# First norm with split row copies and later rounding, and block products one PSUM bank at a time, in a hybrid decoder layer

## What is computed

```
xn = rmsnorm(x, ln1_g)
u, v, q, k, va, ga, gb = split(xn @ w_in)
a = gelu(u) * (tril(W_s[g]) @ rmsnorm(gelu(v)) + b[g])      # chunks of 128, 8 groups
b = sliding-window attention(q, k, va)                      # 16 heads, 4 kv heads, window 128, sinks, ALiBi
x = x + (sigmoid(ga) * (a @ w_oa) + sigmoid(gb) * (b @ w_ob)) @ w_out
x = x + square(relu(rmsnorm(x, ln2_g) @ w_up)) @ w_down
y = rmsnorm(x, lnf_g)
```

## Time and profile before

| | us |
|---|---|
| median of 3 runs | 1611.61 |
| lowest, highest | 1609.47, 1617.08 |
| the profiled execution's own time | 1610.56 |
| its span, first to last instruction | 1608.80 |
| TensorE matmul busy | 1552.6 (97%) |
| VectorE, ScalarE, GpSimd busy | 1054.2, 766.0, 180.6 |

### The profile page before, as it was taken

How to read it: one execution, slowest core, us unless ns; L and a number is a source line. 1 busy time by engine, 2 the same in 40 slices (tenths; PEclk the granted TensorE clock), 3 DMA queues, 4 the chain that set the end, 5 groups by cost and what they waited for, 6 DMA issues and landing times.

```text
span 1608.8 us, 28826 instructions
## 1 busy us (share of the span) xinstructions
PE 1552.6 (97%) x12226; PEld 1516.9 (94%) x12226; DVE 1054.2 (66%) x1377; ACT 766.0 (48%) x1159; POOL 180.6 (11%) x206
## 2 busy tenths in 40 slices
PE   5999999999999989999998999999999999999998
PEld 5988888889999989999998999999999999999997
DVE  4465554312768567866777676977697769776875
ACT  6365555522645535555443555533553355335533
POOL 5122222200000010000110040000000000000001
PEclk7999999999999999999999999999999999999999
DMA  7611110132777614545578363545453636363612
GB/s 223 198 29 53 29 29 27 29 118 79 194 241 222 184 28 106 157 106 157 132 235 186 109 148 102 142 120 143 119 145 109 154 112 151 109 147 112 147 51 106
DMA packets 106409, 200.64 MB, mean 125 GB/s; under 512 B 16624, under 2 KB 44272, under 8 KB 98952
## 3 DMA queue, kind: packets, MB, share of 16 engines
q1 hardware_dynamic: 89344, 127.64, 23.9%
q0 software_dynamic: 10384, 64.00, 20.4%
q10 hardware_dynamic: 6552, 7.13, 1.4%
HBM read 121.77 MB, written 19.30 MB: 88 GB/s over the span
## 4 chain that ended last, share of the span: by engine, by line
PE 85%; DVE 4%; ACT 4%; DMA 3%; issue 2%; POOL 1%; SPq 1%; ACTq 0%; DVEq 0%; POOLq 0%
PE ps L1542 68%; PE ps L1334 10%; PE ps L1322 2%; ACT prob L746 1%; PE ps L1380 1%; DVE prob L1011 1%; DMA h_t<-h_keep 1%; DMA raw<-in_w_in 1%; PE ps L1398 1%; POOL prob L564 1%; DVE y_t L1311 1%; PE ps L1520 1%; DVE w_lo L961 1%; DMA cv<-in_cache_v_win 1%; DVE q_st L991 0%
## 5 line engine op out<-in xcount | busy, mean ns | idle before, releaser
L1542 PE MATMUL ps<-xp_hi,wp_hi 128*128 128x258 f32 x3136 | 634.4, 284 | 6.8 <-DVE wp_lo L1115 6.1
L1542 PE MATMUL ps<-xp_lo,wp_hi 128*128 128x258 f32 x3136 | 635.6, 284 | 0.0
L1542 PE MATMUL ps<-xp_hi,wp_lo 128*128 128x258 f32 x3136 | 634.5, 284 | 0.0
L1542 PEld LDWEIGHTS ps<-xp_hi,wp_hi 128*128 128x128 f32 x3136 | 490.2, 191 | 7.9 <-DVE wp_lo L1115 6.7
L1542 PEld LDWEIGHTS ps<-xp_hi,wp_lo 128*128 128x128 f32 x3136 | 489.8, 190 | 0.0
L1542 PEld LDWEIGHTS ps<-xp_lo,wp_hi 128*128 128x128 f32 x3136 | 486.8, 190 | 0.0
L682 ACT ACTIVATE wp_hi<-wbuf 128x1024 fp32r<-128x1024 f32 x196 | 208.0, 1061 | 549.7 <-PE ps L1542 549.4
L1115 DVE TENSOR_TENSOR wp_lo<-wbuf,wp_hi 128x1024 fp32r<-128x1024 f32 x196 | 243.7, 1243 | 167.1 <-ACT wp_hi L682 167.1
L1334 PE MATMUL ps<-xn_hi,w_hi 128*128 128x344 f32 x480 | 160.8, 335 | 2.5 <-DVE q_st L991 2.5
L1334 PE MATMUL ps<-xn_lo,w_hi 128*128 128x344 f32 x480 | 155.9, 325 | 0.0
L1334 PE MATMUL ps<-xn_hi,w_lo 128*128 128x344 f32 x480 | 155.8, 324 | 0.0
(11 more groups left out here) (191 smaller groups left out, 1555.0 us busy)
## 6 DMA issues: line engine op xcount, KB each, us to landing
wbuf<-wbuf POOLq DMA_DIRECT2D x57, 1024.0 KB, 7.5
wbuf<-in_w_up SPq DMA_DIRECT2D x24, 1024.0 KB, 5.5
wbuf<-in_w_down SPq DMA_DIRECT2D x24, 1024.0 KB, 5.1
wbuf<-in_w_in SPq DMA_DIRECT2D x18, 1024.0 KB, 5.8
raw<-in_w_in SPq DMA_DIRECT2D x40, 256.0 KB, 3.4
wbuf<-in_w_ob SPq DMA_DIRECT2D x6, 1024.0 KB, 7.4
wbuf<-in_w_oa SPq DMA_DIRECT2D x6, 1024.0 KB, 5.0
wbuf<-in_w_out SPq DMA_DIRECT2D x6, 1024.0 KB, 10.8
```

What stands on the lines that cost most here:

```text
L1542: last = mm(ps[:, 2 * p + b, 0:HN], w[:, (2 * n + p // 2) % 2, k, p % 2 * P:(p % 2 + 1) * P], x[n % 2][:, k, b * HN:(b + 1) * HN], start=( ...
```

## The change

In the first norm, tiles go around two pairs of PSUM banks (2 to 5) in place of three (0 to 5). ScalarE copies the first four of a tile's eight blocks and VectorE the other four, with a semaphore of its own that TensorE, GpSimd and the store of `x_t` also wait for. VectorE goes: copy of tile t, scaling of t - 1, `xn_lo` of t - 2. ScalarE goes: square and copy of t, `xn_hi` of t - 2; `w_hi` of job 0 comes one tile earlier. TensorE's spread of a tile comes two tiles after its transposes, and banks 0 and 1 of job 0 are made in halves among the last transposes and spreads. In SyncE's queue `g2`, the sinks and the `raw` pieces of job 1 come after the first three stores. In `product` the loop over the two banks is the outermost.

```diff
+        KA = KT // 2
+        def turned(t):
+            first = 2 + 2 * (t % 2)
+            return ps[:, first:first + 2, :].rearrange("p a (k q) -> p (a k) q", q=P)
...
# SyncE
-            with nc.allow_non_contiguous_dma(reason="gains to partitions, 4 KB each"):
-                for dst, src in ((g2, ln2_g[0]),):
-                    sp.dma_start(dst[:, :], src.rearrange("(k p) -> p k", p=P)).then_inc(small_in, 16)
-            sp.dma_start(nsink[:, :], sinks.to_broadcast([P, H])).then_inc(small_in, 16)
...
+                if g == 0:
+                    for t in range(3):
+                        keep_xn(t)
                 load_block(j + 1, 1 - s, w_in, 0, g * 2 * P + OQ)
                 if g == 0:
-                    for t in range(NTOK):
-                        r = ROWS[t]
-                        sp.wait_ge(xn_ready, t + 1)
-                        sp.dma_start(xn_keep[:, toks(t)].rearrange("(k p) t -> p k t", p=P),
-                                     xg[:, t % 3, :, 0:r]).then_inc(xn_kept[t % 3], 16)
+                    with nc.allow_non_contiguous_dma(reason="gains to partitions, 4 KB"):
+                        sp.dma_start(g2[:, :], ln2_g[0].rearrange("(k p) -> p k", p=P)).then_inc(small_in, 16)
+                    sp.dma_start(nsink[:, :], sinks.to_broadcast([P, H])).then_inc(small_in, 16)
+                    for t in range(3, NTOK):
+                        keep_xn(t)
# GpSimd
                 pool.wait_ge(xt_moved, t + 1)
+                pool.wait_ge(xt_moved_v, t + 1)
# ScalarE
-                copy(x_t[:, :, toks(t)], ps[:, first:first + 2, :].rearrange("p a (k q) -> p (a k) q", q=P)[:, :, 0:r]).then_inc(xt_moved, 1)
-                if t >= 1:
-                    high(t - 1)
-                if t == NBLK - 3:
+                copy(x_t[:, 0:KA, toks(t)], turned(t)[:, 0:KA, 0:r]).then_inc(xt_moved, 1)
+                if t >= 2:
+                    high(t - 2)
+                if t == 4:
                     w_high(0)
+            high(NTOK - 2)
             high(NTOK - 1)
+            act.wait_ge(xt_moved_v, NTOK)
# VectorE
+            def copy_xt(t):
+                dve.wait_ge(xt_done, t + 1)
+                cp(x_t[:, KA:KT, toks(t)], turned(t)[:, KA:KT, 0:ROWS[t]]).then_inc(xt_moved_v, 1)
...
+            for t in range(NTOK):
+                copy_xt(t)
+                if t >= 1:
+                    scale_x(t - 1)
+                if t >= 2:
+                    low(t - 2)
+                if t == 4:
                     split_lo(0, 0)
+            scale_x(NTOK - 1)
+            low(NTOK - 2)
+            low(NTOK - 1)
# TensorE
-                if t >= 3:
-                    spread(t - 3)
-                    pe.wait_ge(xt_moved, t - 2)
+                if t >= 2:
+                    pe.wait_ge(xt_moved, t - 1)
+                    pe.wait_ge(xt_moved_v, t - 1)
                 for k in range(KT):
-                    last = turn(ps[:, first + k // 4, (k % 4) * P:(k % 4) * P + r], x_stage[0:r, t, k * P:(k + 1) * P], r)
+                    last = turn(turned(t)[:, k, 0:r], x_stage[0:r, t, k * P:(k + 1) * P], r)
                 last.then_inc(xt_done, 1)
-            spread(NTOK - 3)
-            pe.wait_ge(xt_moved, NTOK - 2)
-            bank(0, 0, 0, 0, ready=3)
+                if t >= 2:
+                    spread(t - 2)
+                if t >= 7:
+                    bank(0, 0, 0, 0, ready=3, ks=range((t - 7) * KT // 2, (t - 6) * KT // 2))
             spread(NTOK - 2)
+            bank(0, 1, 0, 1, ready=6, ks=range(KT // 2))
             spread(NTOK - 1)
+            bank(0, 1, 0, 1, ks=range(KT // 2, KT))
             pe.wait_ge(xt_moved, NTOK)
+            pe.wait_ge(xt_moved_v, NTOK)
...
-            for n in range(1, 3 * NT):
+            for n in range(2, 3 * NT):
...
-                for k in range(MH):
-                    if p == 0 and k % 2 == 0:
-                        pe.wait_ge(xp_split, 2 * n + k // 2 + 1)
-                    for m, (w, x) in enumerate(passes):
-                        for b in range(2):
+                for b in range(2):
+                    for k in range(MH):
+                        if p == 0 and b == 0 and k % 2 == 0:
+                            pe.wait_ge(xp_split, 2 * n + k // 2 + 1)
+                        for m, (w, x) in enumerate(passes):
                             last = mm(ps[:, 2 * p + b, 0:HN], w[:, (2 * n + p // 2) % 2, k, p % 2 * P:(p % 2 + 1) * P],
```

More of the change, by code:

```diff
@@ L242, in build_trunk @@
         sq_done, rstd_done, rstd_spread = sem("sq_done"), sem("rstd_done"), sem("rstd_spread")
-        xt_done, xt_moved, x_kept = sem("xt_done"), sem("xt_moved"), sem("x_kept")
+        xt_done, xt_moved, xt_moved_v, x_kept = (sem(n) for n in ("xt_done", "xt_moved", "xt_moved_v", "x_kept"))
         xg_done, xn_ready, xhi_done, xn_done = sem("xg_done"), sem("xn_ready"), sem("xhi_done"), sem("xn_done")
@@ L408, in load_block, with keep_xn @@
                 load(j, s, [(raw[:, s, h * KT // 2:(h + 1) * KT // 2, :], halves[h]) for h in (1, 0)])
+            def keep_xn(t):
+                sp.wait_ge(xn_ready, t + 1)
+                sp.dma_start(xn_keep[:, toks(t)].rearrange("(k p) t -> p k t", p=P),
+                             xg[:, t % 3, :, 0:ROWS[t]]).then_inc(xn_kept[t % 3], 16)
             for g in range(NG):
@@ L705, in _ @@
             for t in range(NTOK):
-                r, first = ROWS[t], 2 * (t % 3)
+                r = ROWS[t]
                 act.wait_ge(x_in[t], 16)
@@ L961, in split_lo, with scale_x, low @@
                 tt(w_lo[:, s], raw[:, s], w_hi[:, s].bitcast(F32), ALU.subtract).then_inc(w_split, 1)
-            for t in range(NTOK):
-                r = ROWS[t]
+            def copy_xt(t):
+                dve.wait_ge(xt_done, t + 1)
+                cp(x_t[:, KA:KT, toks(t)], turned(t)[:, KA:KT, 0:ROWS[t]]).then_inc(xt_moved_v, 1)
+            def scale_x(t):
                 dve.wait_ge(xg_done, t + 1)
                 dve.wait_ge(rstd_spread, t + 1)
-                x_ = xg[:, t % 3, :, 0:r]
-                tt(x_, x_, ps[:, 6 + t % 2, 0:r].unsqueeze(1).to_broadcast([P, KT, r]), ALU.mult).then_inc(xn_ready, 1)
+                x_ = xg[:, t % 3, :, 0:ROWS[t]]
+                tt(x_, x_, ps[:, 6 + t % 2, 0:ROWS[t]].unsqueeze(1).to_broadcast([P, KT, ROWS[t]]), ALU.mult).then_inc(xn_ready, 1)
+            def low(t):
                 dve.wait_ge(xhi_done, t + 1)
-                tt(xn_lo[:, :, toks(t)], x_, xn_hi[:, :, toks(t)].bitcast(F32), ALU.subtract).then_inc(xn_done, 1)
-                if t == NBLK - 4:
+                tt(xn_lo[:, :, toks(t)], xg[:, t % 3, :, 0:ROWS[t]], xn_hi[:, :, toks(t)].bitcast(F32), ALU.subtract).then_inc(xn_done, 1)
+            for t in range(NTOK):
[5 more added lines that the diff above has]
+                if t == 4:
                     split_lo(0, 0)
+            scale_x(NTOK - 1)
+            low(NTOK - 2)
+            low(NTOK - 1)
             def bank_low(n):
@@ L1322, in turn, with bank @@
                 return nc.tensor.transpose(out, in_, ident[0:r, 0:r])
-            def bank(j, n, s, b, ready=None):
+            def bank(j, n, s, b, ready=None, ks=range(KT)):
                 if b == 0:
@@ L1331, in bank @@
                     pe.wait_ge(bank_free, n + 1)
-                for k in range(KT):
+                for k in ks:
                     for p, (w, x) in enumerate(((w_hi, xn_hi), (w_hi, xn_lo), (w_lo, xn_hi))):
@@ L1335, in bank @@
                                   start=(k == 0 and p == 0), stop=(k == KT - 1 and p == 2))
-                last.then_inc(bank_done if b < NT - 1 else job_done, 1)
+                if k == KT - 1:
+                    last.then_inc(bank_done if b < NT - 1 else job_done, 1)
             def spread_rstd(place_, t):
```

## The result

The changed kernel takes 1603.64 us, the median of five runs (1599.37 to 1604.26), against 1611.61 (1609.13 to 1617.08) for five of the kernel before: a ratio of 0.9945, with a 95% interval from 0.9927 to 0.9964, or 8.9 us less by the ratio (the medians stand 8.0 apart). The profiled execution took 1599.37 us, its span 1597.6. The forecast was 1606.6 in a range from 1590 to 1618. The gain is 0.55%, with an interval on both sides of 0.5%, so it lies on the edge between the prediction's "same" (0.60) and "faster" (0.30).

A forecast was written before the change was run, and what follows sets the result against it. The prediction took TensorE's own matmul rate as the bound. First norm -4.5, earlier wait +0.5 and loop order 0 gave -4.0 us against the profiled 1610.56: 1606.6 us, in a range from 1590 to 1618.

The forecast's parts named there:

- The products' loop order: Product matmuls (L1542), 9408 steps of 120.5 ns: step time taken as unchanged, 0 us, with -24 and +9 for the range.
- a: Input projection (L1334), 344 columns into one bank: its 14.0 ns surplus would make a product step 121.5 ns, +9 us.
- b: L1380, 256 columns, eight matmuls in two banks with one change of bank: 120.0 ns a step, 120.8 for 258 columns.
- c: Input projection's (L1334) surplus growing with the columns instead: a product step of 118.0 ns, 2.5 cheaper, -24 us.
- one bank is cheaper: Rival on the products' matmuls: smaller surplus per column in one bank, 1583 us at -24 us in full; chance 0.28.
- one bank is dearer: Rival on the products' 9408 steps: 1.0 ns more each, 1615.6 us, or 1625 at twice that; chance 0.10 of passing 0.5%.
- The earlier wait at k = 2: Products: xp_lo's second piece needed after 6 matmuls, not 12, so a covered wait now costs some 0.3 us; +0.5 us.
- The first norm: Norm stage of about 44 us: last scaling 4.5 us sooner, near 39, passing undiminished to job 2; -4.5 us.
- the start: First norm: tile 0's store goes out near 12.3 as small transfers move behind the first three stores; xg of tile 8 2.7 earlier.
- the 7 us that VectorE's own sum promised: First norm: VectorE alone at 3.1 us a tile would end near 37, not 43.6; not taken, because GpSimd shares the port.
- The end: First norm: only tile 6's low part stands before tile 8's scaling, which came 3.3 us after its xg began; 1.8 less.
- the norm isn't shortened: Rival on the first norm: half banks at half clock and moved transfers hold VectorE as long as xn_hi did; 1611, chance 0.14.

The follow-up runs named there:

- order_k_bank_pass: The changed kernel with the products' loops nested k, bank, pass instead of bank, k, pass; 1607.51 us, 120.34 ns a step by the window.
- shifted_operand: The changed kernel with the moving operand's buffer of every second product 32 bytes further on in SBUF; 1599.42 us in one run.
- old_order_one_bank: The changed kernel with the old order of operands and all 24 matmuls of a product part in one bank; 1607.8 us in one run.
- products_only: The kernel before with only the products' new loop order; 1603.64 us in five runs, ratio 0.9956 to the kernel before.
- queue_as_before: The changed kernel with SyncE's queue in the order of the kernel before; 1604.69 us in four runs, ratio 0.9958 to the kernel before.
- one_sbuf_input: The changed kernel with xn_lo's second operand read from PSUM instead of SBUF, so its value is not the low part; 1599.41 us in one run.
- spreads_alone: The changed kernel with the last two tiles' spreads ahead of the half banks in TensorE's queue; 1598.64 us, ratio 0.9933 to the kernel before.
- norm_only: The changed kernel with the products' loops of before put back; 1608.88 us in eleven runs, ratio 0.9989 to the kernel before.

## Why the prediction was right and where it was not

**The products' loop order: 0 predicted, -7.8 us by the step, -7.1 in the total.** This is the term that was mis-sized. The step failed where three readings of other instructions (a, b, c) were taken to bound the price of a bank. They differ in width and in buffers, and by about a nanosecond; in the products, differences of that size came with order and place, as order_k_bank_pass and shifted_operand show, and never with the bank. What makes them in the rows that were read isn't shown. The size lay inside the ends kept (-24 and +9), and on the side of the rival "one bank is cheaper"; but that rival had the wrong mechanism, since one bank alone (old_order_one_bank) gives nothing, and so had "one bank is dearer". The forecast treated the loop order and the bank as one thing and asked only what the bank would cost; the more frequent change of weights stood in it as a reason for a dearer bank alone. Its own sign of being wrong, a step outside 120 to 121 ns, did appear (119.65). What in the order makes the step shorter stays open. The formula cited from the Trainium skill (TensorE: Matmul & The Clock Gate, Back-to-back issue gap), which the page gives for an isolated matmul, makes 110.0 ns a step by estimate; no order that was run comes near it: the lowest is 119.58.

**The earlier wait at k = 2: +0.5 us predicted, 1.1 measured.** In the kernel after, three products have a late seventh matmul, at k = 2, on xp_lo; the largest:

```profile
923.30 0.29 PE L1578 MATMUL ps<-xp_hi,wp_lo 128*128 128x258 f32 x1
923.74 0.39 PE L1578 MATMUL ps<-xp_hi,wp_hi 128*128 128x258 f32 x1
```

```profile
922.46 1.22 DVE L1152 TENSOR_TENSOR xp_lo<-xf,xp_hi 128x1032 fp32r<-128x1032 f32 x1
```

The gap is 0.44 us where 0.12 is a step; the others are 0.37 and 0.32, so 1.13 - 3 x 0.12 = 0.8 us. The step after each is 0.22, which makes 0.3 more. The sign for "wrong" that the prediction set, more than two such waits, did appear. It cost little, and 7.8 - 1.1 = 6.7 us agrees with what products_only measured (7.1).

**The first norm: -4.5 us predicted, -1.8 measured.** By its steps: the start was 2.7 us, by SyncE's queue; it is 2.1 to 2.3, with the store issued at 12.74 instead of 12.3 and landing 1.4 us later than assumed; queue_as_before shows the mechanism. The spacing of the tiles was to stay at 3.63, with xn_lo ending 1.1 us behind each xg; it is 3.71, with 1.08, and one_sbuf_input shows why. The page SBUF — State Buffer of the Trainium skill (Who interferes with whom) is confirmed here, and the 7 us that VectorE's own sum promised were rightly refused. The end was 1.8 us; this step failed. VectorE's share of it came: with the half banks out of the way (spreads_alone) the last scaling starts 1.65 us behind its xg (39.75 and 38.10), against 3.3 before. But the prediction named the half banks ("up to a microsecond") and then left them out of the sum. They hold the last scaling by 0.28 us at 2.4 GHz and by up to 1.79 at 1.2 (norm_only, 3.5 us behind its xg), so it begins between 39.9 and 41.5 and not near 39. The last step, a fixed 18.7 us from the last scaling to job 2, held within 0.2 us in after and norm_only and within 0.6 in the later kernels whose raw is loaded as before.

**The sum** was -4.0 us and is -8.9 by the ratio. Two errors of opposite sign met in it: the products' part was +0.5 and is -7.1, so 7.6 us were missing, and the norm's part had 2.7 too many; 7.6 - 2.7 = 4.9. That the time came out within 3 us of the forecast, well inside the range, is in part luck. The rival "the norm isn't shortened" was nearer to the norm's part than the forecast's own step.

## What to carry to other kernels

In a loop of thousands of back-to-back matmuls, the order in which the operands are streamed is worth trying even where no wait is seen: 0.4% lay in an order of loops here, and the starts per window of the trace show it in one run. The place they are streamed from moved single parts as much, but one shift of 32 bytes won nothing in the mean. When a change alters two things in one edit (bank and order), ask for each alone what it does. Small work that another engine waits for (a spread of 0.4 us) should not stand in TensorE's queue behind a block whose length doubles when the clock is low.

## What the runs showed of the hardware that was not expected

The step of a 258-column matmul at a granted clock of 1.00 is, from start to start, 119.6 to 120.6 ns, according to the order in which the operands are streamed and not to the PSUM bank written; 24 steps differ by up to 16 ns when the moving operand lies 32 bytes further on in SBUF. And a stretch of 3.4 us at half clock, which costs 1.7 us, stands at one place in four of fourteen profiles and is absent from ten: a gain of that size can't be read off one profile of each kernel.
